# A head's attention weights are turned and multiplied one half projection later, and logits alternate between the row halves

## The chip, the core and the metric

The kernel runs on one core of a Trainium2 chip. The core has a matrix engine (TensorE, PE in the rows; its weight loads are listed as PEld), a vector engine (VectorE, DVE), a scalar engine for activations (ScalarE, ACT), a general one (GpSimd, POOL) and a queue engine (SyncE, SP) that here issues the large DMAs. The engines run side by side, each through its own list of instructions in order, and wait for each other by semaphores. The metric is the device time of one execution, in microseconds, lower is better.

## What is computed

One decoder block over 256 tokens of 1024 channels, in float32. The normalised input goes through one wide projection. Its columns feed two mixers: a gated delta rule (linear attention, chunked) and a differential softmax attention with 8 heads. Both outputs are gated, added and projected (w_o); behind that stands an expert network (top 4 of 32 experts). The change touches the differential attention only:

```python
def diff_attention(q, k, v, lam, rel_bias):
    ...
        logits = jnp.einsum('bqhmd,bkhmd->bhmqk', q_blk, k).astype(jnp.float32) * scale
        logits = logits + bias[None, :, None]
        logits = jnp.where(rel[None, None, None] <= 0, logits, -jnp.inf)
        p = jax.nn.softmax(logits, axis=-1)
        attn = p[:, :, 0] - lam * p[:, :, 1]
        return jnp.einsum('bhqk,bkhe->bqhe', attn.astype(v.dtype), v)
```

For each head there are two maps m of logits, over 64 channels each; their two softmaxes are combined to one set of weights, and these multiply the values.

## The kernel before, in words

**Stages.** First the front: the input is normalised and turned, then 24 tiles of the delta mixer's columns are projected with their convolution, then 24 further projections "pj" of 128 tokens by 512 columns (q 0 to 23; four each for QD, KD, VD, Z, GA, GB: attention queries, keys, values, and three sets of gate columns). Each projection is 8 matmuls and is cut in two halves of 4 (L1169), so there are 48 half projections, numbered 0 to 47. Then the gated sum is turned, multiplied by w_o, and the router's plan is made. Last the loop over 32 experts, whose weights come in slabs of 2 MB, six an expert, through a ring of ten places in SBUF.

**The order.** It is written out by hand: `put(i, item)` hangs an item behind half projection i, and `after[i].sort(...)` (L105) sorts the items of one place. From this each engine builds its own list: for each item PE, DVE and ACT run the part that they have in it, in this order, and wait for the others' parts. PE's own items (delta rule steps at L1138, attention steps) thus fill in between half projections. Nothing else decides the order.

**The attention of a head h** has three items:
- `a1`, place 20 + 2h: PE computes logits, L1262 (second query block, 256 keys) and L1263 (first block, 128 keys) for m = 0 and then m = 1; m = 0 lies on partitions 0 to 63, m = 1 on 64 to 127, and each writes a PSUM bank of its own. PE waits for `s_nm`, DVE's taking of the head before. DVE adds the bias and takes the maxima (L970 to L975), ACT makes the exponentials in place (L660, L661).
- `a2`, place 22 + 2h: DVE makes the weights from the exponentials (L980, L983, L985, L988); PE waits for them (`s_aw`) and turns them, 3 blocks (L1271); ACT copies the turned blocks out of PSUM (L668).
- `a3`, place 23 + 2h: PE waits for that copy (`s_aT`) and multiplies the values (L1282, L1283, L1284); ACT squares and copies the result (L674, L675).

Behind each second half of a gate projection (Z: q 12 to 15, GA: 16 to 19, GB: 20 to 23) ACT takes it: for Z a sigmoid and a copy (L648, L651), for GA and GB a sigmoid (L653); DVE multiplies (L961). Exponential and sigmoid need different activation tables (ACT_TABLE_LOAD). From place 20 to 28 there are also delta rule steps: `yt`, `o0`, `qs`, `o1`, and `osum`, DVE's reduction and root of the delta output (L929 to L757) with a square root on ACT (L541). GpSimd squares the delta output (L507) and later multiplies the Z gates by a gain (L510). `odn` at place 38 normalises the attention output, `oan` at place 40 the delta output.

**DMA.** SP issues the projection weights (L374) each when an older piece is used up, then the slabs (L357): the first ten when their ring places are free (`front_dead`), each later one when the slab ten before it is used up.

Of the kernel before, what the change touches and what calls it, by code (L numbers as in the profile page):

```python
# [15 lines left out]
P = 128  # L16
# [20 lines left out]
def block_kernel(nc, x, g_mix, w_in, b_gate, conv_w, a_log, dt_bias, g_delta_out, q_norm, k_norm,  # L37
                 lambda_q1, lambda_k1, lambda_q2, lambda_k2, g_subln, rel_bias, w_o, g_ffn,
                 w_router, b_router, w_up, b_up, w_down, b_down, out):
    _, T, D = x.shape  # L40
# [31 lines left out]
    after = {}  # L72

    def put(i, *its):
        after.setdefault(i, []).extend(its)
# [23 lines left out]
    put(28, ("osum",))  # L99
    for h in range(H):  # L100
        put(20 + 2 * h, ("a1", h))
        put(22 + 2 * h, ("a2", h))
        put(23 + 2 * h, ("a3", h))
    for i in after:
        after[i].sort(key=lambda it: {"a2": 0, "a1": 2}.get(it[0], 1))  # L105
    put(38, ("odn",))
    put(40, ("oan",))

    sched = []
# [17 lines left out]
    with ctx:  # L127
# [612 lines left out]
        def _(dve):  # L740
# [68 lines left out]
            for it in sched:  # L809
# [152 lines left out]
                elif it[0] == "a1":  # L962
                    h = it[1]
                    dve.wait_ge(s_lg, h + 1)
                    if h == 0:
                        dve.wait_ge(s_t5, 16)
                    l = lgt[h % 2]
                    rqv = rq.rearrange("p (b h m) -> p b h m", b=NB, m=2)
                    for m in range(2):
                        v.scalar_tensor_tensor(out=l[:, m, 0:T], in0=pb[:, 4 + m, 0:T], scalar=rqv[:, 1, h, m:m + 1], in1=bias5[:, h, :], op0=ALU.mult, op1=ALU.add)  # L970
                        ins = v.scalar_tensor_tensor(out=l[:, m, T:T + P], in0=pb[:, 4 + m, T:T + P], scalar=rqv[:, 0, h, m:m + 1], in1=bias5[:, h, P:T], op0=ALU.mult, op1=ALU.add)
                    link(ins)
                    v.tensor_reduce(mx[:, h % 2, 0:2], l[:, :, 0:T], AX_X, ALU.max)
                    link(v.tensor_reduce(mx[:, h % 2, 2:4], l[:, :, T:T + P], AX_X, ALU.max))
                    v.tensor_scalar(nmx[:, h % 2], mx[:, h % 2], -1.0, None, ALU.mult).then_inc(s_nm, 1)  # L975
                elif it[0] == "a2":
                    h = it[1]
                    l, r_ = lgt[h % 2], ers[:, h % 2]
                    dve.wait_ge(s_ex, h + 1)
                    link(v.reciprocal(r_, es[:, h % 2]))  # L980
                    if h >= 2:
                        dve.wait_ge(s_atr, h - 1)
                    link(v.tensor_scalar(r_[:, 1:4:2], r_[:, 1:4:2], lamc[:, 0:1], None, ALU.mult))  # L983
                    for j, (lo, hi) in enumerate(((0, T), (T, T + P))):
                        ins = v.tensor_scalar(aw[h % 2][:, lo:hi], l[:, 0, lo:hi], r_[:, 2 * j:2 * j + 1], None, ALU.mult)  # L985
                    link(ins)
                    for j, (lo, hi) in enumerate(((0, T), (T, T + P))):
                        ins = v.scalar_tensor_tensor(out=aw[h % 2][:, lo:hi], in0=l[:, 1, lo:hi], scalar=r_[:, 2 * j + 1:2 * j + 2], in1=aw[h % 2][:, lo:hi], op0=ALU.mult, op1=ALU.add)  # L988
                    ins.then_inc(s_aw, 1)
# [126 lines left out]
        def _(pe):  # L1116
# [24 lines left out]
            for it in sched:  # L1141
# [112 lines left out]
                elif it[0] == "a1":  # L1254
                    h = it[1]
                    if h == 0:
                        pe.wait_ge(s_psBf, 4)
                    else:
                        pe.wait_ge(s_nm, h)
                    for m in range(2):  # L1260
                        rows = slice(64 * m, 64 * m + 64)
                        mm(pb[:, 4 + m, 0:T], atq[rows, h, P:T], atk[rows, h, :], start=True, stop=True)  # L1262
                        ins = mm(pb[:, 4 + m, T:T + P], atq[rows, h, 0:P], atk[rows, h, 0:P], start=True, stop=True)  # L1263
                    ins.then_inc(s_lg, 1)
                elif it[0] == "a2":
                    h = it[1]
                    pe.wait_ge(s_aw, h + 1)
                    if h >= 1:
                        pe.wait_ge(s_aT, h)
                    for k in range(3):  # L1270
                        ins = nc.tensor.transpose(pb[:, 6, k * P:(k + 1) * P], aw[h % 2][:, k * P:(k + 1) * P], ident)  # L1271
                    ins.then_inc(s_atr, 1)
                elif it[0] == "a3":
                    h = it[1]
                    pe.wait_ge(s_aT, h + 1)
                    if h == 0:
                        pe.wait_ge(s_pjf, 24 + no_b[(VD, 1, 1)] + 1)
                    if h >= 2:
                        pe.wait_ge(s_ode, h - 1)
                    val = [vd[:, k, h * P:(h + 1) * P] for k in range(2)]  # L1280
                    o_ = 256 * (h % 2)
                    mm(pb[:, 7, o_ + P:o_ + 2 * P], aT[h % 2][:, 0], val[0], start=True, stop=False)  # L1282
                    mm(pb[:, 7, o_ + P:o_ + 2 * P], aT[h % 2][:, 1], val[1], start=False, stop=True)  # L1283
                    mm(pb[:, 7, o_:o_ + P], aT[h % 2][:, 2], val[0], start=True, stop=True).then_inc(s_od, 1)  # L1284
# [196 lines left out]
```

## Time and profile before

| | us |
|---|---|
| median of 3 runs | 1367.74 |
| lowest and highest | 1364.66, 1368.63 |
| span of the profiled execution | 1365.6 |
| PE busy | 1254.5 (92%) |
| DVE busy | 359.9 (26%) |
| ACT busy | 255.0 (19%) |
| POOL busy | 62.6 (5%) |
| DMA | 453.75 MB, mean 332 GB/s |

Busy shares are means over stages of different kinds. The front ends at about 445 us; from there the expert loop runs to the end. What a change in the front does is read from the engines' order of time in the front, from the rows that say what each wait was for, and from the chain of waits, which tells if the front and the loop hang together. An instruction in the rows is named by its line in the kernel before; "x8" counts records, of which a float32 matmul has two.

### The profile page before, as it was taken

The numbers are of one execution on the slowest core, as the hardware profiler recorded it, in microseconds if no ns is written. First come the engines' busy times: TensorE is split into PE (matmuls) and PEld (weight loads), VectorE is DVE, ScalarE is ACT, GpSimd is POOL, SyncE is SP. The second block draws the span as 40 slices with busy tenths as digits, with TensorE's granted clock in tenths as the row PEclk, the third lists the DMA queues.
The fourth block names the chain that finished last, engine by engine and source line by source line (L and its number), as shares of the span: only waits on it lengthen the run. The fifth ranks groups of instructions, "written<-read, shape, count | busy, mean of one in ns | idle before, by whom it ended". The sixth has DMA issues, their size and how long they took to land.

```text
span 1365.6 us, 14002 instructions
## 1 busy us (share of the span) xinstructions
PE 1254.5 (92%) x5549; PEld 543.3 (40%) x5549; DVE 359.9 (26%) x891; ACT 255.0 (19%) x517; POOL 62.6 (5%) x104
## 2 busy tenths in 40 slices
PE   4969999987998999999999999989999998999997
PEld 3758646643444333333333333333333333333332
DVE  2456773554513112111211111111121111111111
ACT  1423121245312111111111111111111111111110
POOL 5140110001000000000000000000000000000000
PEclk9979999999998999999999999999999999999999
DMA  9653352221359899999999999999999999999995
GB/s 264 116 169 116 93 182 73 99 86 62 124 239 422 335 428 428 428 428 426 428 427 428 428 427 428 428 430 428 426 427 428 429 427 427 429 427 429 428 426 221
DMA packets 59609, 453.75 MB, mean 332 GB/s; under 512 B 12792, under 2 KB 12936, under 8 KB 34752
## 3 DMA queue, kind: packets, MB, share of 16 engines
q1 hardware_dynamic: 53536, 447.76, 79.3%
q0 software_dynamic: 1488, 3.85, 1.6%
q10 hardware_dynamic: 4528, 1.32, 0.5%
q8 instruction: 44, 0.72, 0.2%
q14 instruction: 13, 0.11, 0.0%
HBM read 449.74 MB, written 3.15 MB: 332 GB/s over the span
## 4 chain that ended last, share of the span: by engine, by line
PE 55%; DMA 34%; DVE 6%; ACT 2%; issue 2%; ACTq 0%; SPq 0%; DVEq 0%
DMA ring<-in_w_up_dram 31%; PE pb L1416 15%; PE pb L1452 11%; PE pb L1169 7%; PE pb L1150 4%; PE pb L1371 3%; PE pb L1385 3%; PE pb L1304 2%; DMA gc_rows<-sm 2%; PE pb L1138 2%; PE pb L1377 1%; PE pb L1435 1%; DVE ring L880 1%; DVE ring L879 1%; DVE ring L791 1%
## 5 line engine op out<-in xcount | busy, mean ns | idle before, releaser
L1416 PE MATMUL pb<-ring,buf_a 128*64 128x512 f32 x2048 | 455.8, 596 | 44.5 <-DMA ring<-in_w_up_dram 44.5
L1416 PEld LDWEIGHTS pb<-ring,buf_a 128*64 128x64 f32 x2048 | 143.6, 137 | 338.9 <-issue 247.4
L1452 PE MATMUL pb<-ring,buf_b 128*64 128x512 f32 x1024 | 226.8, 595 | 0.0
L1101 DVE TENSOR_SCALAR buf_a<-pb 128x512 f32<-128x512 f32 x32 | 22.1, 692 | 673.7 <-PE pb L1416 673.7
L1169 PE MATMUL pb<-ring,hT 128*128 128x512 f32 x384 | 176.0, 605 | 0.9 <-PE pb L1169 0.6
L1452 PEld LDWEIGHTS pb<-ring,buf_b 128*64 128x64 f32 x1024 | 70.7, 137 | 131.8 <-issue 127.9
L728 ACT ACTIVATE buf_a<-buf_a 128x512 f32<-128x512 f32 x32 | 20.1, 629 | 471.7 <-DVE buf_a L1101 471.7
L1169 PEld LDWEIGHTS pb<-ring,hT 128*128 128x128 f32 x384 | 71.1, 193 | 80.9 <-issue 80.3
L1150 PE MATMUL pb<-hT,ring 128*128 128x256 f32 x384 | 94.5, 403 | 0.8 <-DVE hT L773 0.8
L1150 PEld LDWEIGHTS pb<-hT,ring 128*128 128x128 f32 x384 | 76.3, 203 | 12.0 <-DVE hT L773 1.2
L1371 PE MATMUL pb<-xt,buf_c 128*64 128x512 f32 x264 | 65.7, 619 | 1.0 <-DVE buf_c L1046 1.0
L1385 PE MATMUL pb<-buf_b 64*128 64x512 f32 x264 | 65.6, 615 | 0.8 <-ACT buf_b L737 0.8
L737 ACT COPY buf_b<-pb 128x512 f32<-128x512 f32 x32 | 18.8, 587 | 234.0 <-PE pb L1452 234.0
L1066 DVE TENSOR_TENSOR buf_a<-pb,sm 128x512 f32<-128x512 f32 x33 | 22.8, 692 | 84.9 <-PE pb L1377 84.9
L728 ACT ACT_TABLE_LOAD x32 | 41.1, 1283 | 1.3 <-issue 0.8
L791 DVE SCALAR_TENSOR_TENSOR ring<-ring,par 128x255 f32<-128x255 f32 (+2 forms) x72 | 38.0, 528 | 2.6
L1371 PEld LDWEIGHTS pb<-xt,buf_c 128*64 128x64 f32 x264 | 16.4, 138 | 44.8 <-issue 44.8
L1138 PEld LDWEIGHTS pb<-ring 128*128 128x128 f32 x240 | 28.7, 192 | 9.8 <-issue 9.8
L1385 PEld LDWEIGHTS pb<-buf_b 64*128 64x128 f32 x264 | 22.8, 186 | 22.5 <-issue 22.5
L1138 PE MATMUL pb<-ring 128*128 128x128 f32 x240 | 29.5, 276 | 2.3 <-DMA ring<-t_blocks 1.9
L1304 PE MATMUL pb<-ring,hT 128*128 128x512 f32 x64 | 28.4, 596 | 1.1 <-ACT hT L681 1.1
L1435 PEld LDWEIGHTS pb<-consts,buf_b 128*128 128x128 f32 x128 | 17.8, 208 | 26.0 <-issue 26.0
(272 smaller groups left out, 809.8 us busy)
## 6 DMA issues: line engine op xcount, KB each, us to landing
ring<-in_w_up_dram SPq DMA_DIRECT2D x128, 2048.0 KB, 40.9
ring<-in_w_down_dram SPq DMA_DIRECT2D x64, 2048.0 KB, 43.4
ring<-in_w_in_dram SPq DMA_DIRECT2D x18, 2048.0 KB, 8.2
ring<-in_w_o_dram SPq DMA_DIRECT2D x2, 2048.0 KB, 8.1
t_rows<-ring POOLq DMA_DIRECT2D x1, 1536.0 KB, 38.5
xt<-in_x_dram SPq DMA_DIRECT2D x2, 512.0 KB, 4.4
ring<-gc_rows ACTq DMA_DIRECT2D x1, 1024.0 KB, 4.8
ring<-t_rows POOLq DMA_DIRECT2D x1, 1024.0 KB, 6.3
```

The costliest lines, as they stand in the source:

```text
L728: sc.activation(sgm, glu, ACT.Sigmoid, scale=ALPHA).then_inc(s_sgm, 1)
L791: ins = v.scalar_tensor_tensor(out=a[:, d:], in0=src[:, 0:T - d], scalar=conv_c[:, 3 - d, tap:tap + 1], in1=a[:, d:], op0=ALU.mult, op1=AL ...
L1066: v.tensor_tensor(xg.rearrange("p (h j) s -> p j h s", h=2), pb[:, 3, :].rearrange("p (j h s) -> p j h s", j=4, h=2), gffn_pairs.rearrange ...
L1138: ins = mm(psA[:, h], lhs(h), rhs(h), start=True, stop=True)
L1150: ins = mm(pb[:, t % 2, 0:T], w[:, c, (t % 4) * P:(t % 4) * P + P], hT[:, c, :], start=(c == 0), stop=(c == KC - 1))
L1169: ins = mm(pb[:, q % 2, :], hT[:, c, b * P:(b + 1) * P], piece_at(n)[:, c, :], start=(c == 0 and g < GA), stop=(c == KC - 1))
L1304: ins = mm(pb[:, 2 + 2 * b + n_, :], mixT[:, c, b * P:(b + 1) * P], piece_at(NPIECE + n_)[:, c, :], start=(c == 0), stop=(c == KC - 1))
L1371: ins = mm(pb[64 * n_:64 * n_ + 64, 3, :], sel[:, b, :], xt[:, b, 512 * n_:512 * n_ + 512], start=(b == 0), stop=(b == NB - 1), skip_group ...
L1385: ins = mm(pb[:, 4 + 2 * b + n_, :], GT[rows, b * P:(b + 1) * P], ys[rows, :], start=False, stop=True, skip_group_check=True)
L1416: ins = mm(pb[64 * hf:64 * hf + 64, n_, :], xg[:, c, :], slot(s)[:, at_:at_ + 512], start=False, stop=(c == KC - 1), skip_group_check=True)
L1435: ins = nc.tensor.transpose(pb[:, j // 2, (j % 2) * P:(j % 2 + 1) * P], act[:, j:512:4], ident)
L1452: ins = mm(pb[64 * hf:64 * hf + 64, 2, :], actT[:, j, hf_in, :], slot(s)[:, at_:at_ + 512], start=(c == 0), stop=(c == KC - 1), skip_group ...
```

## The change

In the schedule each head's second item is split. `aw`, at the old place 22 + 2h, holds only DVE's making of the weights. `a2`, now PE's turn and ACT's copy, moves to 23 + 2h, and `a3`, the product, to 24 + 2h. The sort puts `aw` and `a2` first and `a1` last at a place. `odn` moves from 38 to 39. In `a1` PE issues the 256 wide matmul of both m first, then the 128 wide ones.

```diff
--- before.py
+++ after.py
@@ -99,11 +99,12 @@
     put(28, ("osum",))
     for h in range(H):
         put(20 + 2 * h, ("a1", h))
-        put(22 + 2 * h, ("a2", h))
-        put(23 + 2 * h, ("a3", h))
+        put(22 + 2 * h, ("aw", h))
+        put(23 + 2 * h, ("a2", h))
+        put(24 + 2 * h, ("a3", h))
     for i in after:
-        after[i].sort(key=lambda it: {"a2": 0, "a1": 2}.get(it[0], 1))
-    put(38, ("odn",))
+        after[i].sort(key=lambda it: {"aw": 0, "a2": 0, "a1": 2}.get(it[0], 1))
+    put(39, ("odn",))
     put(40, ("oan",))
 
     sched = []
@@ -973,7 +974,7 @@
                     v.tensor_reduce(mx[:, h % 2, 0:2], l[:, :, 0:T], AX_X, ALU.max)
                     link(v.tensor_reduce(mx[:, h % 2, 2:4], l[:, :, T:T + P], AX_X, ALU.max))
                     v.tensor_scalar(nmx[:, h % 2], mx[:, h % 2], -1.0, None, ALU.mult).then_inc(s_nm, 1)
-                elif it[0] == "a2":
+                elif it[0] == "aw":
                     h = it[1]
                     l, r_ = lgt[h % 2], ers[:, h % 2]
                     dve.wait_ge(s_ex, h + 1)
@@ -1257,10 +1258,11 @@
                         pe.wait_ge(s_psBf, 4)
                     else:
                         pe.wait_ge(s_nm, h)
+                    rows = [slice(64 * m, 64 * m + 64) for m in range(2)]
                     for m in range(2):
-                        rows = slice(64 * m, 64 * m + 64)
-                        mm(pb[:, 4 + m, 0:T], atq[rows, h, P:T], atk[rows, h, :], start=True, stop=True)
-                        ins = mm(pb[:, 4 + m, T:T + P], atq[rows, h, 0:P], atk[rows, h, 0:P], start=True, stop=True)
+                        mm(pb[:, 4 + m, 0:T], atq[rows[m], h, P:T], atk[rows[m], h, :], start=True, stop=True)
+                    for m in range(2):
+                        ins = mm(pb[:, 4 + m, T:T + P], atq[rows[m], h, 0:P], atk[rows[m], h, 0:P], start=True, stop=True)
                     ins.then_inc(s_lg, 1)
                 elif it[0] == "a2":
                     h = it[1]
```

PE, in the halves from projection 13's first half on (lines before: L1169 half projection, L1271 turn, L1262 and L1263 logits, L1282 to L1284 product). Before, with the turn of head 2 in the second row:

```order
L1169 MATMUL pb<-ring,hT 128x512 x4
L1271 MATMUL pb<-consts,ring 128x128 x3
L1262 MATMUL pb<-ring 128x256
L1263 MATMUL pb<-ring 128x128
L1262 MATMUL pb<-ring 128x256
L1263 MATMUL pb<-ring 128x128
L1169 MATMUL pb<-ring,hT 128x512 x4
L1282 MATMUL pb<-ring 128x128
L1283 MATMUL pb<-ring 128x128
L1284 MATMUL pb<-ring 128x128
L1169 MATMUL pb<-ring,hT 128x512 x4
L1271 MATMUL pb<-consts,ring 128x128 x3
```

After, over the same halves (L1170 half projection, L1273 turn, L1263 and L1265 logits, L1284 to L1286 product):

```order
L1170 MATMUL pb<-ring,hT 128x512 x4
L1284 MATMUL pb<-ring 128x128
L1285 MATMUL pb<-ring 128x128
L1286 MATMUL pb<-ring 128x128
L1263 MATMUL pb<-ring 128x256 x2
L1265 MATMUL pb<-ring 128x128 x2
L1170 MATMUL pb<-ring,hT 128x512 x4
L1273 MATMUL pb<-consts,ring 128x128 x3
L1170 MATMUL pb<-ring,hT 128x512 x4
L1284 MATMUL pb<-ring 128x128
L1285 MATMUL pb<-ring 128x128
L1286 MATMUL pb<-ring 128x128
```

The turn of head 2 stood ahead of head 3's logits and now stands behind the half projection after them; the product of head 2 stands one half later too, ahead of head 4's logits.

ACT, from the taking of projection 13 on. Before (L648 and L651 the gate's sigmoid and copy, L674 and L675 the product's square and copies, L668 the copy of the turned weights, L541 the root for `osum`, L660 the exponentials):

```order
L648 ACT_TABLE_LOAD
L648 ACTIVATE ring<-pb 128x512
L651 COPY buf_c<-pb 128x512
L674 ACTIVATE ring,sm<-pb 128x128
L675 COPY buf_a<-pb 128x128
L674 ACTIVATE ring,sm<-pb 128x128
L675 COPY buf_a<-pb 128x128
L668 COPY ring<-pb 128x384
L541 ACT_TABLE_LOAD
L541 ACTIVATE sm<-sm 128x16
L660 ACT_TABLE_LOAD
```

After (L649, L652, L675, L676, L669, L542, L661 in the same parts):

```order
L649 ACT_TABLE_LOAD
L649 ACTIVATE ring<-pb 128x512
L652 COPY buf_c<-pb 128x512
L669 COPY ring<-pb 128x384
L542 ACT_TABLE_LOAD
L542 ACTIVATE sm<-sm 128x16
L675 ACTIVATE ring,sm<-pb 128x128
L676 COPY buf_a<-pb 128x128
L675 ACTIVATE ring,sm<-pb 128x128
L676 COPY buf_a<-pb 128x128
L661 ACT_TABLE_LOAD
```

The copy of turned weights that stood last before the root and the exponentials was head 3's, behind head 2's product; now it is head 2's, directly behind the gate's copy, and head 2's product is squared and copied behind the root. DVE's list is the same in these places; only `odn` stands behind another gate product in it.

## Rows read from the trace of the kernel before

**Rows 1.** Page, part 4: the chain that ended last, shares by engine.
```profile
PE 55%; DMA 34%; DVE 6%; ACT 2%; issue 2%; ACTq 0%; SPq 0%; DVEq 0%
```

**Rows 2.** Chain in order of time: start us, length us, what; its first w_up transfer.
```profile
768.38 40.82 DMA ring<-in_w_up_dram
```

**Rows 3.** Stretches: length, busy PE, PEld, DVE, ACT, POOL (count), PEclk, DMA share, GB/s.
```profile
294.00:296.00 2.00, 2.00 (x3) 0.78 (x3) 1.97 (x6) 0.08 (x1) 0.00 (x0) 0.54 0.00 0
...
445.00:450.00 5.00, 5.00 (x18) 1.48 (x16) 1.05 (x4) 1.28 (x1) 0.00 (x0) 0.56 0.06 23
...
500.00:600.00 100.00, 99.96 (x473) 35.34 (x469) 16.03 (x35) 15.58 (x27) 0.00 (x0) 1.00 1.01 428
```

**Rows 4.** Waits of PE, 250 to 366 us: us in total, times, longest.
```profile
PE pb L1271 <- DVE ring L988: 12.6, 4, 4.3
...
PE pb L1282 <- ACT ring L642: 0.6, 1, 0.6
```

**Rows 5.** PE in order of time: start us, us, instruction, [idle before <-releaser].
```profile
291.71 0.55 PE L1271 MATMUL pb<-consts,ring 128*128 128x128 f32 x3 [3.99 <-DVE ring L988]
...
293.60 4.79 PE L1169 MATMUL pb<-ring,hT 128*128 128x512 f32 x8
...
299.44 3.60 PE L1169 MATMUL pb<-ring,hT 128*128 128x512 f32 x8
303.14 0.55 PE L1271 MATMUL pb<-consts,ring 128*128 128x128 f32 x3
303.62 0.71 PE L1262 MATMUL pb<-ring 64*128 64x256 f32 x4
304.15 0.39 PE L1263 MATMUL pb<-ring 64*128 64x128 f32 x4
304.48 3.70 PE L1169 MATMUL pb<-ring,hT 128*128 128x512 f32 x8
...
308.68 3.60 PE L1169 MATMUL pb<-ring,hT 128*128 128x512 f32 x8
...
332.42 0.55 PE L1271 MATMUL pb<-consts,ring 128*128 128x128 f32 x3 [4.34 <-DVE ring L988]
```

**Rows 6.** ACT in order of time, same columns, head 3.
```profile
292.30 0.48 ACT L668 COPY ring<-pb 128x384 f32<-128x384 f32 x1 [5.00 <-PE pb L1271]
...
296.40 0.51 ACT L660 ACTIVATE ring<-ring,sm 128x256 f32<-128x256 f32 x1 [2.32 <-DVE sm L975]
...
298.28 1.28 ACT L648 ACT_TABLE_LOAD   x1
...
300.06 0.58 ACT L651 COPY buf_c<-pb 128x512 f32<-128x512 f32 x1
```

**Rows 7.** DVE in order of time, head 3 and what follows.
```profile
293.72 0.48 DVE L970 SCALAR_TENSOR_TENSOR ring<-pb,sm,ring 128x256 f32<-128x256 f32 x1 [2.06 <-PE pb L1263]
...
300.68 0.69 DVE L961 TENSOR_TENSOR buf_c<-buf_c,ring 128x512 f32<-128x512 f32 x1 [4.31 <-ACT buf_c L651]
301.29 0.17 DVE L980 RECIPROCAL sm<-sm 128x4 f32<-128x4 f32 x1
...
303.01 2.28 DVE L929 TENSOR_REDUCE sm<-ring 128x16 f32<-128x2048 f32 x1
...
306.90 0.48 DVE L970 SCALAR_TENSOR_TENSOR ring<-pb,sm,ring 128x256 f32<-128x256 f32 x1
```

**Rows 8.** DVE (L907, L961) and POOL in order of time, heads 2 and 5.
```profile
287.08 1.21 DVE L907 TENSOR_TENSOR buf_b<-buf_b,pb 128x1024 f32<-128x1024 f32 x1
...
325.83 0.69 DVE L961 TENSOR_TENSOR buf_c<-buf_c,ring 128x512 f32<-128x512 f32 x1 [4.32 <-ACT buf_c L651]
...
288.37 1.89 POOL L507 TENSOR_TENSOR ring<-buf_b 128x1024 f32<-128x1024 f32 x1 [14.75 <-DVE buf_b L907]
326.60 4.63 POOL L510 TENSOR_TENSOR buf_c<-buf_c,consts 128x1024 f32<-128x1024 f32 x2 [36.33 <-DVE buf_c L961]
```

**Rows 9.** SP in order of time: the first slabs issued.
```profile
388.98 2.18 SPq L357 DMA_DIRECT2D ring<-in_w_up_dram  x4
```

## The prediction

> **What bounds the kernel now.** I read the chain of work that ended last first. By engine it is 55% TensorE (PE) and 34% DMA [rows 1], and these lie one behind the other: the first piece of the chain that is a weight transfer in the expert loop starts at 768.38 us [rows 2]; up to there it is nearly all matmuls. The stretches say how the two are joined. At 445 to 450 us, where the expert loop begins, the DMA moves 23 GB/s, later 428 without a pause [rows 3]. The ten ring places are full as the loop begins, and the transfers resume when the loop's first slab has been used. From there the stream never stops, so the end is that moment plus a fixed number of bytes. That moment is set by PE, in order, through the whole front. **A microsecond taken out of PE's front is a microsecond of the total**; the gap of some 5 us moves along with it.
>
> In the front, PE's waits in the attention stretch are 12.6 us on L988, VectorE's (DVE's) last step of a head's weights, and 0.6 us of head 0's product on a value copy [rows 4]. Three of them, 4.0 us (twice) and 4.3, make up nearly all; they stand at L1271, the turning of heads 2, 4 and 5, the first at 291.71 and the last at 332.42 us [rows 5]. After a wait the granted clock falls: 0.54 in 294 to 296 us [rows 3]. Each fall to the lower of the two levels (1.2 GHz) shows in the half projection behind it: 4.79 us where an undisturbed one is 3.7 [rows 5] (1.1 us), and in the turn and logits ahead of it: 291.71 to 293.60 is 1.89 us, 303.14 to 304.48 is 1.34 (0.55). That is 1.7 us each. So all that the old waits cost is 12.6 + 0.6 + 3 x 1.7 = 18.3 us.
>
> **Why DVE is late.** Head 3 at its undisturbed durations [rows 6, 7]: bias and maximum 293.72 to 296.40 (2.68 us), exponentials on ScalarE (ACT) to 298.28 (1.88), table load, gate sigmoid and gate copy to 300.64 (2.36), gate product 0.61, weights from 301.29 to about 303.09 (1.80). That is 9.4 us from logits to weights; PE's own two half projections with all three attention steps take 299.44 to 308.68, 9.24 us [rows 5]. Two of the three waits are longer because GpSimd runs: its 1.89 us product lies in head 2's weights, and its 4.63 us pair in head 5's, where gate product to turn takes 325.83 to 332.42, 6.59 us [rows 5, 8], against 300.68 to 303.14, 2.46 us, for head 3. Head 4's wait is the reduction and root of the delta output ahead of its bias and maximum on DVE, 303.01 to 306.90, 3.9 us [rows 7].
>
> **What the change removes.** DVE's order stays. PE meets the turn one half projection later, about 3.5 us plus 0.9 of the logits that now go before it: 4.4 us of room against waits of 4.0, 4.0 and 4.3. Also the next head's logits no longer stand behind a late turn, so DVE can go on with them at once. The turn's three matmuls and the product's three are the same instructions, so no work is added.
>
> **What it adds.** ACT's copy of the turned weights used to stand ahead of the exponentials. Now it stands behind the next head's exponentials, the table load and the gate's sigmoid and copy, and PE needs it for the product only one half projection after the turn. Behind that product on PE stand the next logits and so everything. The new loop is: logits 0.86, bias and maximum 2.68, exponentials 1.88, load to gate copy 2.36, turned copy 0.48, product 0.7, and about 0.3 of handing over: 9.3 us, against PE's own 9.24 [rows 5 to 7]. So the loop is level with PE when nothing disturbs it, and each disturbance of DVE's chain comes out as a wait at L1284, for ACT. I walk it through with the durations above, by adding each to the later of its two predecessors (times on the old profile's axis):
> - Up to head 2's logits PE doesn't wait: the 0.6 us goes, and a turn and a product move behind the state step, so DVE's chain of head 2 runs 0.6 + 0.5 + 0.7 = 1.8 us ahead.
> - Head 2's weights meet GpSimd again and end at 289.8 instead of 291.7. PE has done head 3's logits; DVE takes them at once: 292.5, exponentials 294.4, gate copy 296.6, turned copy 297.1. PE comes to head 2's product at 294.8 and **waits 2.5 us**. Head 4's logits start at 298.0 instead of 303.6.
> - Head 3's weights 299.1, reduction and root 303.0, head 4's bias 305.7, exponentials 307.6, gate copy 309.9, turned copy 310.4. PE comes at 306.4 and **waits 4.1 us**. Head 5's logits start at 311.2 to 311.9 instead of 317.2.
> - Head 4's product has no wait. Head 5's weights start behind a gate product at 320.7, meet the 4.63 us pair and end at 327.7. Its turn **waits 0.8 us**, DVE then does head 6's bias to 330.4, exponentials 332.3, sigmoid 334.1, turned copy 334.6; PE comes to head 5's product at 331.9 and **waits 2.8 us**. Head 7's logits start at about 335.9 instead of 344.0.
> - Behind that nothing waits.
>
> New waits are 2.5 + 4.1 + 0.8 + 2.8 = 10.2 us; each chain step that hands over a tenth faster than I walk it shortens them, down to 8.6. I take 9.3 against the old 13.2: **3.9 us** less waiting. The clock: the fall behind the first new wait is covered by the second wait and costs nothing, that behind the second by the head without a wait, half at most; that behind the last costs its 1.7 us if it comes. So of 5.1 us there remain 0 to 2.5; I take 0.9 and book **4.2 us**. Together **8.1 us**, with bounds 3.0 + 2.6 = 5.6 and 4.6 + 5.1 = 9.7. The walk's end says the same: head 7's logits start 8.1 us earlier, and behind them only the clock can differ.
>
> **The alternation of row halves.** The old order is 256, 128, 256, 128 columns, the first two on the one half of the rows. In the trace all four records of the 256 wide line start before any of the 128 wide line (303.62 against 304.15), and the four together take 303.62 to 304.48, 0.86 us [rows 5]. At the projection's 3.5 us for 4 matmuls of 512 columns, 384 columns are 0.66 us: the two halves already run side by side. So I put it at nothing; the bounds are 0 and 0.2 us a head, 1.6 in all, of which half would be hidden in front of waits.
> The Trainium skill, "TensorE: Matmul & The Clock Gate", Part 3 (packing small matmuls), says that matmuls keep program order in start and end. By that rule the second half's 256 columns could not start ahead of the first half's 128, the old order would be the longer, and alternation would gain some 0.2 to 0.4 us a head by an estimate from the rule; the measured 0.86 us leaves no room for this.
> The Trainium skill, "ScalarE: Activation LUTs", What ACT_TABLE_LOAD costs, gives 2.66 us for a switch, load and drain together. The row has 1.28 us, and the copy behind the sigmoid starts 0.5 us after it [rows 6]; the measurement decides. By the page the new loop would be 1.4 us longer a head, and the sum some 4 us smaller.
>
> **The closing normalisation** of the attention output moves one half projection later (place 39) and on ACT and DVE behind the last GA gate. It delays DVE's first output product by some 6 us; PE asks for that product only after all four GB projections, two halves of some 3.5 us each [rows 5], 28 us in all; the two normalisations and the product take DVE some 14 us. The rest is cover. SP's queue: the slabs, of which some wait for the last head's output, are issued from 388.98 us [rows 9], behind a w_o piece that waits for projection 22 of 24; the last head's product is in projection 19. Nothing is on the path.
>
> **The sum.** 1365.6 of the span - 8.1 = 1357.5; the three runs' median is 2.1 us above the profiled span, so 1359.6 us.
>
> **Rivals.** (1) *The new waits at the product aren't there*, because ACT is earlier than I walk it: then all 18.3 us go, 1349.4 us. Against it: the loop of 9.3 us, and the three disturbances, which the change doesn't touch. 5%.
> (2) *The same waits, more of them*: GpSimd's products catch a second DVE step, or every gate head pays some 0.7 us in the loop that I call level. Each costs 2 to 4 us; the gain is 2 to 6, the time 1361.7 to 1365.7. 15%.
> (3) *The end doesn't follow the front*: if the stream of slabs were continuous before 445 us, an earlier loop would only wait for data: 1367.7. The 23 GB/s stretch speaks against it. 6%.
> (4) *Slower*: ACT's turned copy, queued behind sigmoids that themselves wait for PE and DVE, makes PE wait at every product. It decides from an average of 18.3 / 7 = 2.6 us for heads 1 to 7; at head 3's 4.1 us for all of them it is 29 us of waits, some 10 us slower, 1378. 4%.
>
> **How the numbers follow.** Forecast 70%, its own range 1356.5 to 1362.5: the bounds of the sum, 1358.0 and 1362.1, with part of the runs' scatter below. A measurement here can tell about 0.3%, 4.1 us, from no change, so faster means under 1363.6: 0.70 of the forecast, 0.05 of (1), and half of (2), 0.82. Same: the rest of (2) and (3), 0.14. Slower 0.04. The range 1355.5 to 1364.0 leaves out (1), (3), (4) and the end of (2), some 0.2.
>
> **What would show it.** Right: waits on L988 almost gone (at most 1 us, head 5); new waits at L1284 on ACT's L669 copy, 2 to 5 us each, for heads 2, 3 and 5; logits of 0.86 us as before; the expert loop starting near 437 us and the DMA gap the same length. Wrong: PE's waits under 3 us in all (rival 1), waits at L1284 for six heads or more (rivals 2 and 4), or a loop that starts earlier and ends at the old time (rival 3).

## The result, and the profile after

| | before | after |
|---|---|---|
| median, us | 1367.60 (4 runs) | 1354.88 (4 runs) |
| lowest and highest | 1364.66, 1368.63 | 1353.17, 1355.49 |
| profiled span | 1365.6 | 1351.2 |

The ratio is 0.9904, with a 95% interval of 0.9888 to 0.9921: 12.7 us less. The forecast was 8.1 us less, 1359.6, with a range that ended at 1355.5; the time fell 0.6 us below it. The direction and the mechanism came out, the size didn't. In a second series, beside other runs of before, the changed kernel took 1356.55 against 1367.91, 11.4 us less.

PE's waits in the attention stretch of the changed kernel (us in total, times, longest), which answer to [rows 4]:

```profile
PE pb L1284 <- ACT ring L669: 7.0, 3, 4.0
PE pb L1273 <- PE pb L1170: 0.9, 3, 0.3
```

No wait on DVE's weights is left. There are three waits on ACT's copy of the turned weights (L669) at the product (L1284); the 0.3 us ones are PE waiting for its own last matmul, and stand in the old order too. PE in order of time (start, length, instruction, idle before and releaser), to be read beside [rows 5]:

```profile
290.15 3.60 PE L1170 MATMUL pb<-ring,hT 128*128 128x512 f32 x8
295.23 0.49 PE L1284 MATMUL pb<-ring 128*128 128x128 f32 x2 [1.48 <-ACT ring L669]
...
308.41 0.80 PE L1284 MATMUL pb<-ring 128*128 128x128 f32 x2 [4.00 <-ACT ring L669]
...
311.57 4.71 PE L1170 MATMUL pb<-ring,hT 128*128 128x512 f32 x8
...
321.64 0.70 PE L1263 MATMUL pb<-ring 64*128 64x256 f32 x4
...
331.98 0.49 PE L1284 MATMUL pb<-ring 128*128 128x128 f32 x2 [1.51 <-ACT ring L669]
...
332.85 0.70 PE L1263 MATMUL pb<-ring 64*128 64x256 f32 x4
```

The waits stand at the products of heads 2, 3 and 5, 1.48, 4.00 and 1.51 us, where the walk had put 2.5, 4.1 and 2.8. Behind the second, a half projection takes 4.71 us. From the logits of a head to the half projection behind them it is 0.86 us as before (321.64 to 322.50). The last row is the start of head 7's logits.

ACT at head 3's product, in order of time, beside [rows 6]: head 4's exponentials start, then the table load, the gate's sigmoid and copy, and last the turned copy, which PE takes at 308.41.

```profile
303.73 0.51 ACT L661 ACTIVATE ring<-ring,sm 128x256 f32<-128x256 f32 x1 [1.41 <-DVE sm L976]
...
305.61 1.28 ACT L649 ACT_TABLE_LOAD   x1
306.90 0.60 ACT L649 ACTIVATE ring<-pb 128x512 f32<-128x512 f32 x1
307.40 0.58 ACT L652 COPY buf_c<-pb 128x512 f32<-128x512 f32 x1
307.86 0.50 ACT L669 COPY ring<-pb 128x384 f32<-128x384 f32 x1
```

DVE, and one row of POOL: the reduction for the delta output's root (L930), behind it head 4's bias (301.05), and the gate product, weights and next bias around GpSimd's pair, beside [rows 7, 8].

```profile
297.16 2.28 DVE L930 TENSOR_REDUCE sm<-ring 128x16 f32<-128x2048 f32 x1
...
301.05 0.48 DVE L971 SCALAR_TENSOR_TENSOR ring<-pb,sm,ring 128x256 f32<-128x256 f32 x1
...
318.65 0.69 DVE L962 TENSOR_TENSOR buf_c<-buf_c,ring 128x512 f32<-128x512 f32 x1 [4.32 <-ACT buf_c L652]
...
319.47 2.33 DVE L984 TENSOR_SCALAR sm<-sm 128x2 f32<-128x2 f32 x1
321.83 2.59 DVE L986 TENSOR_SCALAR ring<-ring,sm 128x256 f32<-128x256 f32 x2
...
325.12 0.48 DVE L971 SCALAR_TENSOR_TENSOR ring<-pb,sm,ring 128x256 f32<-128x256 f32 x1
...
319.42 4.65 POOL L511 TENSOR_TENSOR buf_c<-buf_c,consts 128x1024 f32<-128x1024 f32 x2 [32.86 <-DVE buf_c L962]
```

From the reduction to head 4's bias it is again 3.9 us, and GpSimd's 4.65 us pair lies again in head 5's weights: a step on 2 columns takes 2.33 us. Gate product to the end of the weights is 318.65 to 325.1, 6.5 us. All three disturbances are where they were; only what they reach is different.

The chain of waits still meets its first w_up transfer far behind the front (start, length, what; beside [rows 2]):

```profile
753.18 41.02 DMA ring<-in_w_up_dram
```

### The profile page after: what moved, and what is told of

Read it like the earlier page. It is cut to its first block, busy times and chain, and to the rows that moved or that the text cites. A ratio compares the mean times of both kernels' runs of the same rounds, so it can differ in the third digit from the quotient of the medians.

```text
span 1351.2 us, 14002 instructions
## 1 busy us (share of the span) xinstructions
PE 1245.0 (92%) x5549; PEld 540.1 (40%) x5549; DVE 356.3 (26%) x891; ACT 254.6 (19%) x517; POOL 62.9 (5%) x104
## 4 chain that ended last, share of the span: by engine, by line
PE 56%; DMA 34%; DVE 5%; ACT 2%; issue 1%; ACTq 1%; SPq 0%; DVEq 0%
DMA ring<-in_w_up_dram 32%; PE pb L1418 15%; PE pb L1454 11%; PE pb L1170 8%; PE pb L1151 5%; PE pb L1373 3%; PE pb L1387 3%; DMA gc_rows<-sm 2%; PE pb L1306 2%; PE pb L1139 2%; PE pb L1379 1%; PE pb L1437 1%; DVE ring L881 1%; DVE ring L880 1%; PE pb L1427 1%
## 5 line engine op out<-in xcount | busy, mean ns | idle before, releaser
L1170 PE MATMUL pb<-ring,hT 128*128 128x512 f32 x384 | 174.3, 600 | 1.0 <-PE pb L1170 0.7
L1170 PEld LDWEIGHTS pb<-ring,hT 128*128 128x128 f32 x384 | 70.2, 191 | 79.2 <-issue 78.3
L1151 PEld LDWEIGHTS pb<-hT,ring 128*128 128x128 f32 x384 | 74.7, 198 | 11.4 <-DVE hT L774 1.2
L1437 PEld LDWEIGHTS pb<-consts,buf_b 128*128 128x128 f32 x128 | 17.8, 209 | 26.0 <-issue 26.0
```

The costliest lines, as they stand in the source:

```text
L1151: ins = mm(pb[:, t % 2, 0:T], w[:, c, (t % 4) * P:(t % 4) * P + P], hT[:, c, :], start=(c == 0), stop=(c == KC - 1))
L1170: ins = mm(pb[:, q % 2, :], hT[:, c, b * P:(b + 1) * P], piece_at(n)[:, c, :], start=(c == 0 and g < GA), stop=(c == KC - 1))
L1437: ins = nc.tensor.transpose(pb[:, j // 2, (j % 2) * P:(j % 2 + 1) * P], act[:, j:512:4], ident)
```

## Where the time went, stretch by stretch

The trace gives three joints that every kernel here has: the first logits, the first turning of the mixed output (the end of the projections), and the issue of the first w_down slab that waits for a freed place in the expert loop. Before:

```profile
396.48 1.07 PE L1294 MATMUL pb<-consts,buf_a 128*128 128x128 f32 x8 [0.30 <-PE pb L1169]
...
445.32 15.95 PE L1416 MATMUL pb<-ring,buf_a 128*64 128x512 f32 x64
...
451.01 3.76 SPq L357 DMA_DIRECT2D ring<-in_w_down_dram  x2
```

After:

```profile
385.19 1.06 PE L1296 MATMUL pb<-consts,buf_a 128*128 128x128 f32 x8 [0.30 <-PE pb L1170]
...
432.16 13.91 PE L1418 MATMUL pb<-ring,buf_a 128*64 128x512 f32 x64
...
435.81 3.76 SPq L358 DMA_DIRECT2D ring<-in_w_down_dram  x2
```

With the same three joints from all profiles (us; "attention" is the first logits to the first turning, "entry" from there to the freed slab, "loop" from there to the end):

| kernel | first logits | attention | entry | loop |
|---|---|---|---|---|
| before | 251.7 | 144.7 | 54.5 | 914.6 |
| e1, alternation only | 251.0 | 146.7 | 50.5 | 914.5 |
| e5, before with entry filled | 248.1 | 145.2 | 49.6 | 914.6 |
| e11, before with waits filled | 250.2 | 142.7 | 50.6 | 914.5 |
| after | 249.9 | 135.3 | 50.6 | 915.4 |
| after_again | 251.3 | 135.3 | 51.1 | 914.9 |
| e2, later turn only | 251.0 | 135.3 | 50.9 | 914.7 |
| e4, after with entry filled | 250.2 | 135.3 | 51.3 | 914.6 |
| e12, after with wait filled | 251.5 | 135.6 | 54.2 | 914.6 |
| e8, gain left out | 251.9 | 133.6 | 54.7 | 914.6 |
| e6, product later | 253.6 | 133.3 | 50.9 | 914.6 |
| e3, root late | 250.9 | 130.0 | 50.9 | 914.6 |
| e9, root late, entry filled | 248.8 | 131.6 | 49.6 | 914.7 |
| e10, all three | 252.5 | 129.4 | 49.6 | 914.3 |

Between the two profiled executions lie 14.4 us: 1.8 ahead of the attention, 9.5 in it, 3.9 in the entry, and the loop is 0.8 longer.

Three things are to be seen. **The loop is a constant**: 914.3 to 915.4 us in 14 profiles, whatever stands ahead of it. So the end follows the freed slab, as the prediction said. **The attention stretch is worth 10.3 us**: 145.5 on average in the three profiles with the old order and nothing filled in it, 135.3 in the three with the new one (four with e4). **The entry varies from profile to profile** by 4 us for kernels that are alike in it, and so does what lies ahead of the attention, by 5.5 us (248.1 to 253.6). The granted clock (the number behind the last count) names the first of these. Before, two stretches ahead of those in [rows 3]:

```profile
435.00:440.00 5.00, 3.06 (x13) 1.06 (x13) 4.16 (x20) 0.59 (x4) 0.00 (x0) 0.58 1.04 439
440.00:445.00 5.00, 5.00 (x18) 1.55 (x16) 2.10 (x14) 0.96 (x2) 0.00 (x0) 0.50 1.01 429
```

It is at the lower level (1.2 GHz) from about 436 to 449 us. After:

```profile
425.00:430.00 5.00, 4.07 (x11) 0.96 (x11) 3.88 (x19) 0.67 (x2) 0.00 (x0) 0.66 1.01 429
430.00:435.00 5.00, 4.93 (x27) 2.16 (x28) 2.54 (x14) 1.66 (x2) 0.00 (x0) 1.00 0.84 357
```

There the fall is over at 430. e8, whose entry is the changed kernel's to the instruction, has the long fall again:

```profile
425.00:430.00 5.00, 4.02 (x14) 1.15 (x15) 3.89 (x19) 0.41 (x3) 0.00 (x0) 0.50 1.00 426
430.00:435.00 5.00, 5.00 (x16) 1.79 (x16) 1.49 (x10) 1.22 (x3) 0.00 (x0) 0.50 0.86 367
435.00:440.00 5.00, 5.00 (x18) 1.46 (x16) 1.05 (x4) 1.00 (x1) 0.00 (x0) 0.63 0.01 3
```

## The experiments

All edits are on the kernel before or the changed one, as said. "Less" is the distance of the medians, against the runs of before from the same series. The ratio weighs all single runs and not the two medians, and can stand up to 2 us from that distance; its interval is what a difference has to clear.

**Alternation alone (e1)**, on the kernel before:

```diff
-                    for m in range(2):
-                        rows = slice(64 * m, 64 * m + 64)
-                        mm(pb[:, 4 + m, 0:T], atq[rows, h, P:T], ...)
-                        ins = mm(pb[:, 4 + m, T:T + P], atq[rows, h, 0:P], ...)
+                    rows = [slice(64 * m, 64 * m + 64) for m in range(2)]
+                    for m in range(2):
+                        mm(pb[:, 4 + m, 0:T], atq[rows[m], h, P:T], ...)
+                    for m in range(2):
+                        ins = mm(pb[:, 4 + m, T:T + P], atq[rows[m], h, 0:P], ...)
```

> The kernel before with the row halves alternating and nothing else moved. Theory A (the two row halves already ran side by side, so the gain is all from the later turn): logits of a head take 0.86 us on PE from start to start as before, PE's waits of about 13 us stay, and the time is that of before within 1 us, ratio 0.9993 to 1.0007. Rival B (alternation lets the halves overlap for the first time): 0.66 us or less a head and 1.6 us or more gained, ratio 0.9988 or lower.

Measured: 1367.38 against 1367.78, ratio 1.0004 (0.999 to 1.0017). PE in order of time, the logits of head 0 up to the half projection behind them:

```profile
251.00 0.70 PE L1262 MATMUL pb<-ring 64*128 64x256 f32 x4
251.53 0.39 PE L1264 MATMUL pb<-ring 64*128 64x128 f32 x4
251.85 1.55 PE L1169 MATMUL pb<-ring,hT 128*128 128x512 f32 x3
```

It is 0.85 us, as with the old order, where the trace had put the records in the same sequence. Rival B's 0.9988 is outside the interval. Alternation is worth nothing that can be measured.

**The later turn alone (e2)**: the changed kernel with the old order of the logits, the diff above read backwards.

> The changed kernel with the logits in the old order of row halves; only the turn and the product are later. Theory A: all of the change's gain, 12.7 us, ratio 0.9895 to 0.9915, with the same three waits at the product (1.5, 4.0, 1.5 us). Rival B: the gain of the change less 1.6 us or more, ratio 0.992 or higher.

Measured: 1354.08, 13.7 us less, ratio 0.9912 (0.9891 to 0.9933), 7.1 us of waits on the turned copy in three waits, attention 135.3. The interval alone would still leave room for rival B; with e1's it doesn't, since alternation by itself gained nothing. So the gain is that of the later turn together with the product behind it; no run moves the one without the other.

**The root out of head 4's chain (e3)**, on the changed kernel:

```diff
-    put(28, ("osum",))
+    put(37, ("osum",))
```

> The changed kernel with the reduction and root of the delta output moved from place 28 to place 37, out of head 4's chain on DVE and ACT. Theory (the 4.0 us wait at head 3's product is that step, 3.9 us, passed on through head 4's bias, exponentials and the gate's sigmoid): that wait falls under 1 us, the fall of the clock behind it goes, and the time is 4 to 6.5 us below the changed kernel's, about 1349.5. Rival (ACT's own order, table load, sigmoid and copy ahead of the turned copy, makes the wait whatever DVE does): a wait of 3 us or more stays and the time falls by less than 1.5 us.

Measured: 1349.98, ratio 0.9885 (0.9861 to 0.991), 17.8 us less, that is 4 to 5 us below the changed order (e2's median in the same series, and the changed kernel's in the first table). PE's waits at products are these two:

```profile
296.20 0.49 PE L1284 MATMUL pb<-ring 128*128 128x128 f32 x2 [1.48 <-ACT ring L669]
...
327.68 0.49 PE L1284 MATMUL pb<-ring 128*128 128x128 f32 x2 [2.23 <-ACT ring L669]
```

The wait of 4.0 us at head 3's product is gone, no fall of the clock is left in this profile's attention, and attention is 5.3 us shorter. Head 5's wait has grown from 1.5 to 2.2: part of the lead is given back at the next disturbance. The theory holds: the wait is the root's 3.9 us, handed on by DVE and ACT.

**GpSimd's pair taken away (e8)**, on the changed kernel. It leaves out the gain of seven delta heads, so it computes less.

```diff
-                pool.tensor_tensor(gz_h[:, b], gz_h[:, b], gdor[:, None, :].to_broadcast([P, H, P]), ALU.mult)...
+                pool.tensor_tensor(gz_h[:, b, 0], gz_h[:, b, 0], gdor, ALU.mult)...
```

> The changed kernel; GpSimd multiplies the Z gate by the gain for the first delta head only and leaves the other seven out, so its 4.65 us pair shrinks to under 1 us. Theory (the 1.5 us wait at head 5's product is that pair in DVE's weights of head 5, passed on through head 6's bias): the weights of head 5 take 1.8 instead of 5.9 us, the wait goes, and the time falls by only 1.5 us, since the rest of the 4.1 us has cover. Rival (a collision with GpSimd costs its full length on the path): 4 us less.

Measured: 1356.35, which is 10.0 us less than before and so no gain over the changed kernel. But the waits are two, 5.5 us (below), not three, 7.0, and attention is 1.7 us shorter, as the theory had it. The profile has its entry 4.0 us longer than the changed kernel's, by the long fall of the clock shown above. The trace settles the wait; the time can't, since the entry's scatter is larger.

```profile
PE pb L1284 <- ACT ring L669: 5.5, 2, 4.0
```

**The product later still (e6)**, on the changed kernel:

```diff
-        after[i].sort(key=lambda it: {"aw": 0, "a2": 0, "a1": 2}.get(it[0], 1))
+        after[i].sort(key=lambda it: {"a3": -1, "aw": 0, "a2": 0, "a1": 2}.get(it[0], 1))
...
-        put(24 + 2 * h, ("a3", h))
+        put(25 + 2 * h, ("a3", h))
...
-    put(39, ("odn",))
+    put(40, ("odn",))
```

The sort puts the product ahead of the next head's turn. In a first form without that line, nothing kept PE's write of a PSUM bank behind ACT's reading of it, so that form has no time.

> The changed kernel with the product of each head another half projection later (place 25 + 2h, sorted ahead of the next turn; the closing normalisation at 40). Theory (what is left is PE waiting for ACT's turned copy one half projection after the turn): the waits at the product vanish; the disturbances of DVE's chain then reach PE only at the turn, which has 4.4 us of room, so waits of 0 to 3 us in all instead of 7.0, no fall of the clock, 4 to 9 us below the changed kernel, 1346 to 1351. Rival (the loop over DVE and ACT sets the pace and PE waits elsewhere for as long): waits of 5 us or more at the turn and the time within 2 us of the changed kernel.

Measured: 1354.19, ratio 0.9914 (0.9895 to 0.9933), 12.2 us less: nothing over the changed kernel. PE's waits (us in total, times, longest):

```profile
PE pb L1273 <- DVE ring L989: 2.4, 2, 2.1
PE pb L1263 <- DVE sm L976: 1.2, 1, 1.2
PE pb L1284 <- ACT ring L669: 1.0, 1, 1.0
```

They are about 4.5 us, on two steps of DVE and one of ACT, instead of 7.0, with two falls of the clock of 3.4 us each instead of one of 6.8, and attention is 2.0 us shorter. My expectation of 4 to 9 us was wrong, and the rival's "as long elsewhere" is nearer: with the copy's limit gone the disturbances come out at the turn, at the logits (which wait for DVE's maximum of the head before) and once still at the product.

**The entry filled (e4, e5)**, three matmuls that nothing reads, in PE's idle times ahead of the loop; e4 is the changed kernel, e5 the one before:

```diff
+            keep = consts[:, 0:4, :].rearrange("p i j -> p (i j)")
+            for _ in range(2):
+                mm(pb[:, 2, :], ident, keep, start=True, stop=True)
             pe.wait_ge(s_cho, NB)
...
+            mm(pb[:, 2, :], ident, keep, start=True, stop=True)
             pe.wait_ge(s_sel, 1)
             gather()
```

> The changed kernel with three matmuls of 512 columns added that nothing reads, two in front of PE's wait for the expert choice (1.9 us of idle time) and one in front of its wait for the token selection (1.0 us). Theory (how long the clock stays low at the entry of the expert loop differs from execution to execution, 3.4 to 13.7 us in the profiles so far, because of these two idle times): no fall of the clock between the last projection and the loop, the stretch from the first turning of the mixed output to the first freed slab falls from 50.6 to about 49 us, and the time by 1.7 us or more, with less scatter. Rival (the falls there have another cause): the fall stays and the time too.

> The kernel before with the same three added matmuls. Theory (part of the change's 12.7 us is that the changed kernel meets a shorter low clock at the loop's entry, the attention itself is worth 9.5 to 11.4): 2 to 5 us less than before, about 1364, and the distance to the changed kernel with the same matmuls is 9.5 to 11.4 us. Rival (the entry has no part in it): the distance is 12.7 us or more.

Measured: e5 1362.39, ratio 0.9975 (0.9962 to 0.9989), 4.0 us less; e4 1351.29, 15.1 us less. Both are faster without any work being saved, and their distance is 11.1 us. e5's profile has no fall at the entry and an entry of 49.6 us. e4's still has one of 3.4 us, and 51.3 us where 49 were expected; so the fill doesn't rule the fall out. That it shortens the falls can be read from the granted clock of the single runs: on average 0.987 over e5's 12 runs against 0.983 over the 17 of before beside them, and 0.9905 over e4's six where the changed kernel has 0.985 and 0.986. The distance of 11.1 lies between the theory's 11.4 and 9.5, but the intervals are wide enough for the rival's 12.7 too.

**PE's waits filled (e11, e12)**, with four such matmuls each. e11 is the kernel before, ahead of the turns of heads 2, 4 and 5 (into the turned blocks' PSUM bank, behind the wait for its last copy); e12 the changed kernel, ahead of head 3's product:

```diff
+                    if h in (2, 4, 5):
+                        for _ in range(4):
+                            mm(pb[:, 6, :], ident, consts[:, 0:4, :]..., start=True, stop=True)
                     pe.wait_ge(s_aw, h + 1)
```

> The kernel before with four matmuls of 512 columns that nothing reads (3.5 us) in front of PE's waits for the weights of heads 2, 4 and 5, so that PE isn't idle in the three waits of 4.0 to 4.3 us. Theory (the clock term of the prediction: each of the three falls costs 1.7 us on the path): no fall between 280 and 345 us and 5.1 us less, about 1362.5. Rival (a slow stretch lies in front of the next wait, which takes part of it back): no fall either, but only 1.5 to 3 us less, and new waits of 0.5 to 1 us at the turns of heads 3, 6 and 7.

> The changed kernel with four such matmuls in front of PE's wait at head 3's product, 4.0 us long. Theory (the one fall there costs what is not taken back by the next wait): no fall between 300 and 320 us, a wait of 0.5 to 1 us at head 4's product in its place, and 1 to 2 us less. Rival (the fall's 2.6 us, half of the 5.2 us after PE resumes, are all on the path): 2.6 us less.

Measured: e11 1361.60, ratio 0.9967 (0.9951 to 0.9983), 5.7 us less; its profile has no fall in the attention, which is 142.7 us, 2.8 less than the old order's average. Its waits on the weights, in order of time:

```profile
290.25 0.55 PE L1274 MATMUL pb<-consts,ring 128*128 128x128 f32 x3 [0.58 <-DVE ring L988]
...
301.24 0.52 PE L1274 MATMUL pb<-consts,ring 128*128 128x128 f32 x3 [1.31 <-DVE ring L988]
...
314.33 0.55 PE L1274 MATMUL pb<-consts,ring 128*128 128x128 f32 x3 [0.55 <-DVE ring L988]
...
329.37 0.55 PE L1274 MATMUL pb<-consts,ring 128*128 128x128 f32 x3 [1.41 <-DVE ring L988]
...
339.88 0.52 PE L1274 MATMUL pb<-consts,ring 128*128 128x128 f32 x3 [0.86 <-DVE ring L988]
...
350.37 0.52 PE L1274 MATMUL pb<-consts,ring 128*128 128x128 f32 x3 [0.32 <-DVE ring L988]
```

Heads 3, 6 and 7 now wait 1.31, 0.86 and 0.32 us, as the rival said: a faster PE comes too early at the next turn. Beside the profile of before, whose three falls cost 1.7 us each, 2.1 of the 5.1 us reach the end of the stretch. In the whole time the interval is 2.3 to 6.7 us, so the 5.7 of the medians and the 2 to 3 of the stretch don't contradict each other. e12: 1354.46, 12.9 us less, and attention 135.6 us: nothing gained. There the fall behind head 3's product is gone, and this is what came for it:

```profile
296.77 0.49 PE L1287 MATMUL pb<-ring 128*128 128x128 f32 x2 [1.48 <-ACT ring L669]
...
309.95 0.49 PE L1287 MATMUL pb<-ring 128*128 128x128 f32 x2 [0.56 <-ACT ring L669]
...
332.16 0.49 PE L1287 MATMUL pb<-ring 128*128 128x128 f32 x2 [2.23 <-ACT ring L669]
```

From the first logits to head 5's product it is 80.7 us, against 82.1 in the changed kernel: of the 2.6 us that the fall had cost, 0.56 and 0.7 went into the waits at heads 4 and 5, and 1.4 were gained up to there. Then head 5's wait, now 2.23 us instead of 1.51, is followed by a fall of 3.4 us that the changed kernel's isn't, and that takes the 1.4 back. So the theory's price of 1 to 2 us was right up to head 5's product; the time shows nothing of it.

What a fall costs with no wait behind it is seen by accident in two profiles whose attention is alike to the instruction (e3, and e9 below). Both wait 2.23 us at head 5's product. Behind it, e9's granted clock is 0.50 from 326 to 328 us and e3's 1.00 from 328 to 330, and e9's attention is 1.6 us longer. The logits behind the wait show it, e9 first:

```profile
325.58 0.49 PE L1284 MATMUL pb<-ring 128*128 128x128 f32 x2 [2.23 <-ACT ring L669]
...
326.80 1.23 PE L1263 MATMUL pb<-ring 64*128 64x256 f32 x4
```

In e3 the same logits, behind the product at 327.68 shown above:

```profile
328.55 0.70 PE L1263 MATMUL pb<-ring 64*128 64x256 f32 x4
```

**The changed kernel again, and the combinations (e9, e10)**: e9 is the changed kernel with the diffs of e3 and e4, e10 has e6's as well.

> The changed kernel once more, beside the next two and more runs of before. If the change's gain is 10 to 11.4 us of attention plus a part at the loop's entry that comes and goes with the clock, the distance is 11 to 14 us, and the profile has three waits at the product of 1.5, 4.0 and 1.5 us again, whatever the fall at the entry is.

> The changed kernel with the root of the delta output at place 37 and the three matmuls in PE's idle times ahead of the loop. If both causes are separate, their effects add: 4 to 5 us from the root and 2.5 to 3.5 from the entry, 1346 to 1348. If the one only takes what the other gives, it stays at 1350.

> The same with the product one more half projection later as well. The later product alone took 2 us out of the attention stretch but the time stayed; with the root out of the way its two falls of the clock should go too. If so, 2 to 3.7 us below the kernel with warm and root alone; if the waits it leaves at the turn and at the logits are GpSimd's and stay, within 1.5 us of it.

Measured: 1356.55 for the changed kernel (11.4 less, ratio 0.9921, 0.9897 to 0.9946); e9 1348.59, ratio 0.987 (0.9848 to 0.9892), 19.3 us less; e10 1348.03, ratio 0.9863 (0.9839 to 0.9887), 19.9 us less. The changed kernel's three waits are there again, 6.7 us. Root and entry add, roughly: e9 is 8.0 us below the changed kernel of the same series, where 6.5 to 8.5 were expected. The later product adds 0.6 us, which is inside the scatter, and not the 2 to 3.7 expected: a wait of 2.3 us at a turn is left and a fall of the clock behind it. e9 and e10 beat both kernels; between the two, e9 has the simpler order.

## Why the prediction came out as it did

The mechanism held; the step that failed is the size of the term "new waits". It was walked at 10.2 us, bounded by 8.6 and booked at 9.3, and the waits are 6.9. With it the waiting saved was 5.8 us and not 3.9, outside that term's own bounds of 3.0 to 4.6. The table has the sum's terms beside the averages of the profiles (us; three old, three new):

| | booked | measured |
|---|---|---|
| waits saved | 3.9 | 5.8 |
| clock | 4.2 | 3.8 (estimate, point 4) |
| neither of them | 0 | 0.7 |
| attention in all | 8.1 | 10.3 |
| the whole time | 8.1 | 12.7 and 11.4 |

1. **What bounds the kernel**: right. The loop is 914.3 to 915.4 us in every profile, and 5 us less of attention (e3) is 4 to 5 us less in all. Rival 3 is out.
2. **The old waits go, new ones come at the product, for ACT's copy**: right, and at the three heads that the walk named. e3 and e8 show two of the three causes by taking them away; head 2's, GpSimd's square of the delta output, wasn't taken away and rests on its rows.
3. **The size of the new waits**: the term that failed. They are 6.9 us on average (7.0, 7.1, 6.7). Put on one axis by the first logits (1.8 us), the walk's times of ACT's copies were right to 0.1 us for head 2 (297.1 against 297.0) and to 0.2 for head 3 (310.4 against 310.2) and late by 0.9 for head 5 (334.6 against 333.7), of which 0.5 is that I gave the disturbed weights 6.4 us and not the 5.9 that lie between gate product's end and turn in [rows 5, 8]. And PE came 0.8 us later to head 2's product and 0.4 later to head 5's than I had it; 0.3 of each is a wait for its own last matmul (at 289.80 and 316.58), which I left out. A wait is the difference of two sums of 15 to 30 us, so errors of under 1 us in either make a third of it. The predicted 0.8 us at head 5's turn, a difference of that kind, isn't there at all. The end of the walk was nearer than its waits: head 7's logits start at 334.7 on the old axis (332.85 in the trace), and the walk had 335.9.
4. **The clock term**: 4.2 us booked, and the total fits by luck. I estimate from the traces what PE lost by it as half of its busy time at the lower level, in stretches of 0.5 us: 5.1, 7.8 and 6.5 us in the three profiles with the old order, 2.6, 2.9 and 2.5 in the three with the new one. I had booked 5.1 and 0.9. So both were too low, the old since two of the three profiles have falls of 6.8 us beside the 3.4 that I saw, and the new since the one fall there is 6.8 us long; the difference is 3.8. And such a loss isn't what taking the fall away gives: e11 and e12 show 2.1 of 5.1 us and 1.4 of 2.6 reaching PE behind the next waits, e9 beside e3 all of it where no wait follows. That last is what the prediction had said of a fall behind the last wait.
5. **The entry of the loop**: taken as fixed, without a reason. It is 50.5 to 54.7 us for the same instructions, by the length of the fall behind PE's two idle times. The profile that I summed from had the long one and the changed kernel's a short one, which is 3.9 of the 14.4 us between these two. That the change has a part in it isn't shown: over all profiles with nothing filled there, the old order averages 51.9 us (54.5, 50.5, 50.6) and the new one 51.9 too (50.6, 51.1, 50.9, 54.2, 54.7, 50.9, 50.9).
6. **Alternation**: right, worth nothing (e1, e2). **The closing normalisation**: right, no wait for it showed up.

The range failed by its lower end. I had drawn it from the bounds of the two terms, and the attention alone gained more (10.3 us) than the upper bound of their sum, 9.7. There was also no allowance for the entry, though [rows 3] showed the clock at 0.56 where the loop begins.

What stays open: the 2.4 us between the attention's 10.3 and the 12.7 of the medians. A part can be scatter: the second series has 11.4, the two kernels with the entry filled lie 11.1 apart. A part can be that the two profiled executions of the old order without any fill had a granted clock of 0.985 and 0.984, where the old kernel's runs average 0.983, so that a usual execution has longer falls than these profiles; no profile of such an execution was taken. Open too is what makes one fall 3.4 us long and another 13.7 behind the same idle times.

## What to carry to other kernels

When a step is moved behind others on one engine, look at what moves behind others on its partner: here the weights got 4.4 us of room, but the copy of the turned block came to stand behind the next head's exponentials and a gate's sigmoid, and three waits came back at the next consumer. Take a wait from a walk as the difference of two sums, give it the errors of both, and don't book the full price of a slow clock if another wait follows, since a faster engine then waits longer there. Split the span at a few joints that all variants share: single runs of the changed kernel scatter by 6 us (1352.4 to 1358.6) and hid a gain of 1.7, while the attention stretch of that order was 135.3 us in all four profiles. But compare all profiles that are alike in a stretch, not the two that come first: the entry seemed to give 3.9 us and gives nothing in the average.

## What the runs showed of the hardware

- The granted clock behind the same short idle times was low for 3.4, 6.8 or 13.7 us in different profiles of the same instructions at the loop's entry, and the stretch was up to 4 us longer. Three matmuls without use, 2.6 us of work in idle time, made the kernel before 4.0 us faster by the medians (ratio 0.9975, 0.9962 to 0.9989).
- The same wait of 2.23 us at head 5's product was followed by a fall of 3.4 us in e9 and e12 and by none in e3.
- In the changed kernel, at head 3's wait of 4.0 us, the clock had fallen before PE resumed: 0.50 in both stretches from 308 to 312 us (start:end, length, busy times, clock in the third number from the right):

```profile
308.00:310.00 2.00, 1.59 (x8) 1.37 (x8) 1.89 (x6) 0.36 (x1) 0.00 (x0) 0.50 0.00 0
310.00:312.00 2.00, 2.00 (x10) 1.60 (x10) 0.72 (x3) 1.89 (x7) 0.00 (x0) 0.50 0.00 0
```

- Two row halves of the array took 0.86 us for 384 columns each in either program order, with both 256 wide matmuls recorded ahead of both 128 wide ones even where the program has them otherwise.
- A DVE step on 128 x 2 elements (L984) took 2.33 us while GpSimd multiplied, and 0.23 us without.
